# Attention: score rows of the second block folded to their 128 visible columns by a predicated copy, and the transposed blocks parted by GpSimd

## The reference

```python
qi = jnp.arange(WINDOW)[:, None]              # WINDOW = 128
kj = jnp.arange(2 * WINDOW)[None, :]
rel = qi + WINDOW - kj
sc = jnp.einsum('bqkgd,bjkd->bkgqj', qx, kx) * scale
valid = (rel >= 0) & (rel < WINDOW) & (blk * WINDOW + kj - WINDOW >= 0)
sc = jnp.where(valid[None, None, None], sc, NEG_INF)
p = jax.nn.softmax(jnp.concatenate([sc, sink_logits], axis=-1), axis=-1)[..., :-1]
return jnp.einsum('bkgqj,bjkd->bqkgd', p.astype(vx.dtype), vx)
```

## Time and profile before

| | us |
|---|---|
| median of three runs | 1015.26 (1015.19 to 1015.81) |
| the profiled execution | 1015.4 |
| its span, first to last instruction | 1013.6 |
| TensorE busy | 1009.5 |
| VectorE busy | 786.3 |
| ScalarE busy | 497.2 |
| GpSimd busy | 101.4 |

### The profile page before, as it was taken

One profiled execution on the slowest core, in us unless ns is written; L12 is line 12 of the kernel. 1 busy time (PEld: TensorE's weight loads), 2 busy tenths in 40 slices (PEclk: granted clock), 3 DMA queues, 4 the chain that ended last, 5 costly groups with the idle time before them and its releaser, 6 DMA issues.

```text
span 1013.6 us, 15818 instructions
## 1 busy us (share of the span) xinstructions
PE 1009.5 (100%) x5916; PEld 886.5 (87%) x5916; DVE 786.3 (78%) x886; ACT 497.2 (49%) x537; POOL 101.4 (10%) x103
## 2 busy tenths in 40 slices
PE   9999999999999999999999999999999999999998
PEld 8888888888888888888888888888897898888888
DVE  7988866797797878777767787787778977977743
ACT  7455435544443354454444454464447944544432
POOL 0000013201101052000013100001220041000000
PEclk9999999999999999999999999999999999999999
DMA  9664456652542454555455645535562344644461
GB/s 348 242 237 177 143 174 218 246 197 104 218 195 97 193 171 173 212 190 180 150 179 199 246 166 201 191 135 172 187 244 115 110 160 188 208 168 166 156 193 64
DMA packets 32295, 185.31 MB, mean 183 GB/s; under 512 B 3840, under 2 KB 6400, under 8 KB 16128
## 3 DMA queue, kind: packets, MB, share of 16 engines
q1 hardware_dynamic: 31968, 184.64, 50.9%
q10 hardware_dynamic: 288, 0.16, 0.1%
HBM read 183.73 MB, written 1.05 MB: 182 GB/s over the span
## 4 chain that ended last, share of the span: by engine, by line
PE 100%; DVE 0%; issue 0%; DVEq 0%
PE ps L1219 99%; PE ps L1585 1%; PE ps L1552 0%; PE ps L1544 0%; DVE x L841 0%; DVE ones L1125 0%; DVEq L1126 0%
## 5 line engine op out<-in xcount | busy, mean ns | idle before, releaser
L1219 PE MATMUL ps<-h,w_hi 128*128 128x512 f32 x1664 | 556.1, 393 | 0.0
L1219 PE MATMUL ps<-h,w_lo 128*128 128x256 f32 x1664 | 430.8, 279 | 0.0
L658 DVE TENSOR_TENSOR w_lo<-stage,w_hi 128x2048 fp32r<-128x2048 f32 (+1 forms) x190 | 398.2, 2105 | 29.3 <-ACT w_hi L339 29.1
L1219 PEld LDWEIGHTS ps<-h,w_hi 128*128 128x128 f32 x1664 | 310.1, 188 | 66.9 <-DVE w_lo L658 0.2
L339 ACT ACTIVATE w_hi<-stage 128x2048 fp32r<-128x2048 f32 (+1 forms) x190 | 326.7, 1727 | 5.6 <-PE ps L1219 4.7
L1219 PEld LDWEIGHTS ps<-h,w_lo 128*128 128x128 f32 x1664 | 302.1, 189 | 3.5
L1219 PE MATMUL ps<-act_t,w_hi 128*128 128x512 f32 (+1 forms) x726 | 240.0, 386 | 0.0
L1219 PE MATMUL ps<-act_t,w_lo 128*128 128x256 f32 x704 | 190.1, 279 | 0.0
L1219 PEld LDWEIGHTS ps<-act_t,w_hi 128*128 128x128 f32 x726 | 134.4, 188 | 28.4
L371 ACT ACTIVATE tmp<-ps 128x1024 f32<-128x1024 f32 x44 | 45.1, 1026 | 189.2 <-PE ps L1219 189.2
L1219 PEld LDWEIGHTS ps<-act_t,w_lo 128*128 128x128 f32 x704 | 130.4, 189 | 0.3
(11 more groups left out here) (172 smaller groups left out, 746.9 us busy)
## 6 DMA issues: line engine op xcount, KB each, us to landing
stage<-w_in_dram SPq DMA_DIRECT2D x85, 1024.0 KB, 4.8
stage<-w_out_dram SPq DMA_DIRECT2D x64, 704.0 KB, 4.0
stage<-w_ret_dram SPq DMA_DIRECT2D x24, 1024.0 KB, 4.9
stage<-w_ret_out_dram SPq DMA_DIRECT2D x8, 1024.0 KB, 4.8
stage<-w_q_dram SPq DMA_DIRECT2D x4, 1024.0 KB, 6.3
stage<-w_o_dram SPq DMA_DIRECT2D x4, 1024.0 KB, 4.9
stage<-w_in_dram SPq DMA_DIRECT2D x8, 256.0 KB, 4.2
stage<-w_in_dram SPq DMA_DIRECT2D x2, 512.0 KB, 6.1
```

Source lines behind the costliest of these rows:

```text
L658: nc.vector.tensor_tensor(w_lo[:, s, 0:n], stage[:, s, 0:n], w_hi[:, s, 0:n].bitcast(F32), ALU.subtract).then_inc(lo_ready, 1)
L1219: return nc.tensor.matmul(out_, w, x_, start=start, stop=stop)
```

## The change

In the second block a query sees exactly one of the two keys at each position modulo 128. Now the scores of both blocks are computed without a mask product, and VectorE copies, where the old mask of the own block is not zero, the score of the earlier block over that of the own block: a predicated copy in PSUM. Maximum, exponential, scaling and transposes then work on 128 columns a head instead of 256. The transposed block is copied by ScalarE to the second half of `pt_two`; GpSimd multiplies it with a 0/1 triangle to get the part that belongs to the earlier block, and subtracts that from the whole to get the other part. The value products stay as they were, but wait for GpSimd (`p_second`) and not for ScalarE. The first half of the mask constant becomes the 0/1 triangle.

```diff
-    s_two = [at(f"s_two{c}", [P, CH, 2 * P], F32, (big + 20480, base + 110592)[c]) for c in range(2)]
+    s_two = [at(f"s_two{c}", [P, CH, P], F32, (big + 20480, base + 110592)[c]) for c in range(2)]
...
+    def row_scores(e, j):
+
+        return scores(e, j)[:, keys(e) - P:keys(e)]
...
-                    nc.scalar.activation(s[:, j, :], scores(e, j), ACT.Exp, bias=sm[:, e, 1, j:j + 1],
+                    nc.scalar.activation(s[:, j, :], row_scores(e, j), ACT.Exp, bias=sm[:, e, 1, j:j + 1],
...
-                first = h0 + heads * r
+                first = h0 + 4 * r
...
-                nc.scalar.activation(pt[:, first:first + heads, :, :],
-                                     ps[:, P_T_BANKS[e][r], :].rearrange("p (a k n) -> p a k n", a=heads, n=P),
+                nc.scalar.activation((pt_two if b else pt_own)[:, first:first + 4, b, :],
+                                     ps[:, P_T_BANKS[e][r], :].rearrange("p (a n) -> p a n", n=P),
                                      ACT.Copy).then_inc(pt_ready[e][r], 1)
...
...
-                chain.step(nc.vector.tensor_reduce(mx.rearrange("q (i p) -> q i p", p=2), scores_by_head(e), AX.X,
-                                                   ALU.max))
+                by_head = scores_by_head(e)
+                if b:
+                    chain.step(nc.vector.copy_predicated(
+                        by_head[:, :, :, P:2 * P],
+                        mask[:, P:2 * P].bitcast(I32).rearrange("q (i p k) -> q i p k", i=1, p=1).broadcast_to(
+                            [P, n // 2, 2, P]), by_head[:, :, :, 0:P]))
+                    by_head = by_head[:, :, :, P:2 * P]
+                chain.step(nc.vector.tensor_reduce(mx.rearrange("q (i p) -> q i p", p=2), by_head, AX.X, ALU.max))
...
+            def blocks_of_p(n, e):
+
+                c, b, h0, heads = SOFTMAXES[e]
+                first, second = (pt_two[:, h0:h0 + heads, kb, :] for kb in range(2))
+                pool.wait_ge(pt_ready[e][0], 1)
+                nc.gpsimd.tensor_tensor(first, second, same(mask[:, 0:P], heads), ALU.mult).then_inc(p_first, 1)
+                pool.wait_ge(p_first, n + 1)
+                nc.gpsimd.tensor_tensor(second, second, first, ALU.subtract).then_inc(p_second, 1)
+
+            pool.wait_ge(mask_loaded, 48)
             pool.wait_ge(rope_loaded, 32)
...
             square_sum(ATT)
+            for n, e in enumerate((TWO_0A, TWO_0B, TWO_1A, TWO_1B)):
+                blocks_of_p(n, e)
             square_sum(5)
...
-                                  False, j >= h0 + n - 2)
+                                  bool(b), bool(b) or j >= h0 + n - 2)
...
-                    pe.wait_ge(pt_ready[e][0], 1)
-                    pe.wait_ge(pt_ready[e][1], 1)
+                    pe.wait_ge(p_second, 2 * c + k % 2 + 1)
...
-                masks(TWO_0A)
-                masks(TWO_0B)
-                transposed_p(TWO_0A, 1)
-                transposed_p(TWO_0B, 1)
-                pe.wait_ge(pt_ready[TWO_0B][0], 1)
-                pe.wait_ge(pt_ready[TWO_0B][1], 1)
-                masks(TWO_1A)
-                pe.wait_ge(pt_ready[TWO_0A][1], 1)
                 transposed_p(OWN_0, 1)
+                pe.wait_ge(pt_ready[TWO_0B][0], 1)
                 head_scores(TWO_1A)
-                masks(TWO_1B)
-                transposed_p(TWO_1A, 1)
-                pe.wait_ge(pt_ready[TWO_1A][1], 1)
-                transposed_p(TWO_1B, 1)
...
+    mask[:, 0:P] = np.arange(P)[:, None] > np.arange(P)[None, :]
```

More of the change, by code:

```diff
@@ L234, in trunk @@
     p_scaled, p_ready = sem("p_scaled"), sem("p_ready")
+    p_first, p_second = sem("p_first"), sem("p_second")
     pt_done, pt_ready = ([[sem(f"{n}{e}{r}") for r in range(2)] for e in range(len(SOFTMAXES))]
@@ L548, in rows_of_p @@
                 c, b, h0, n = SOFTMAXES[e]
-                pt = pt_two if b else pt_own
-                heads = 4 // (1 + b)
-                first = h0 + heads * r
+                first = h0 + 4 * r
                 if c:
@@ L582, in attention @@
                 rows_of_p(TWO_0A, 0)
-                rows_of_p(TWO_0A, 1)
                 rows_of_p(TWO_0B, 0)
-                rows_of_p(TWO_0B, 1)
                 squares(1, 1)
@@ L599, in attention @@
                 rows_of_p(TWO_1A, 0)
-                rows_of_p(TWO_1A, 1)
                 rows_of_p(OWN_1, 1)
@@ L604, in attention @@
                 rows_of_p(TWO_1B, 0)
-                rows_of_p(TWO_1B, 1)
                 split(v + 1)
@@ L1055, in softmax_back @@
                 nc.vector.tensor_tensor(
-                    s, s, sm[:, e, 4, h0:h0 + n].rearrange("p (g a) -> p g a", a=1).broadcast_to([P, n, keys(e)]),
+                    s, s, sm[:, e, 4, h0:h0 + n].rearrange("p (g a) -> p g a", a=1).broadcast_to([P, n, P]),
                     ALU.mult).then_inc(p_ready, 1)
@@ L1558, in masks @@
                 c, b, h0, n = SOFTMAXES[e]
-                own = mask_r[:] if b else mask_r[:, P:2 * P]
                 for bank in SCORE_BANKS[e]:
-                    matmul(ps[:, bank, 0:n // 2 * keys(e)].rearrange("p (a n) -> p a n", a=n // 2), ident_r[:],
-                           same(own, n // 2), True, False)
+                    matmul(ps[:, bank, :].rearrange("p (a n) -> p a n", a=n // 2), ident_r[:],
+                           same(mask_r[:, P:2 * P], n // 2), True, False)
             def head_scores(e):
@@ L1582, in transposed_p @@
                 for q in range(4):
-                    tile = 4 * r + q
-                    head, kb = (tile // 2, tile % 2) if b else (tile, 0)
                     last = nc.tensor.transpose(ps[:, P_T_BANKS[e][r], q * P:(q + 1) * P],
-                                               s[:, h0 + head, kb * P:(kb + 1) * P], ident[:])
+                                               s[:, h0 + 4 * r + q, :], ident[:])
                 last.then_inc(pt_done[e][r], 1)
```

## The result

The changed kernel took 1024.80 us (median of 6 runs, 1023.88 to 1029.43) against 1015.22 (1014.93 to 1015.81) for the kernel before in the same comparison: ratio 1.0098, interval [1.0087, 1.0109]. It is slower; 1023.5 had been forecast. Five of the six runs lie between 1023.88 and 1024.98; the profiled one is the sixth, 1029.43, with a span of 1027.6 us, so its trace holds some 5 us that the typical run does not.

What follows compares the result with a forecast made beforehand. TensorE was taken as busy nearly throughout, with VectorE also at its limit in the attention stage. Holds and waits from GpSimd, less saved transposes, summed to +8.2 us on the profiled 1015.4: 1023.5 us predicted, range 1019 to 1026.

Steps and rivals of the forecast that it cites:

- What bounds the stage: Attention stage: up to the first output tile TensorE can't run ahead of VectorE, so work removed there turns into waiting.
- rival C: Attention stage: the whole removed TensorE work pays, 1011.8 us; chance 0.04.
- B: Rival at the value products: GpSimd's pair of operations is hidden, not slower, -0.5 us, 1014.9; chance 0.07.
- A: Rival: no exclusion between GpSimd and VectorE, only GpSimd's latency counts, +0.8 us, 1016.2; chance 0.12.
- D: Rival: only TWO_1A and TWO_1B cost, where splits collide with GpSimd; +5.3 us, 1020.7; chance 0.77 together with the forecast.
- place 1: TWO_0A and TWO_0B: GpSimd holds VectorE's rope addition and OWN_0 multiplication, +3.1 us, delaying the first output tile.
- VectorE's part of the fold: Four fronts: predicated copy 0.68 us added, maximum halved from 1.22 to 0.69, +0.2 us a front.
- Place 2: TWO_1A: two GpSimd operations and VectorE's split share the port; TensorE's value products wait 3.0 us.
- Place 3: TWO_1B: GpSimd's operations and VectorE's splits hold each other; TensorE's value products wait 2.8 us.
- the sum: Attention stage: +3.1 + 0.2 - 0.44 + 3.0 - 0.44 + 2.8 = +8.2 us on the profiled 1015.4.

Runs made afterwards that it cites:

- e6: Kernel before with the eight mask products of the second block's softmaxes left out, scores unmasked: 1015.73 us, ratio 1.0002.
- e1: Changed kernel without GpSimd's eight operations; value products take the whole transposed block for both key blocks: 1015.42 us, ratio 0.9999.
- e2: Changed kernel with GpSimd's eight operations going into a tile nobody reads, value products not waiting for them: 1019.84 us, ratio 1.0041.
- e0: Changed kernel run again, unedited: 1023.83 us, ratio 1.0093 against the kernel before.
- e3: Changed kernel with 35 unneeded mask products filling TensorE's four waits: 1024.13 us, ratio 1.0085.
- e9: Changed kernel with another VectorE order behind TWO_1B, the last two output divisions each ahead of a split: 1020.62 us, ratio 1.0052.
- e5: Changed kernel with VectorE multiplying from PSUM, GpSimd making only the difference of the value blocks, used as weight: 1017.86 us, ratio 1.0021.
- e4: Changed kernel with GpSimd only multiplying, the subtraction moved into the value products: 1019.18 us, ratio 1.0040.

## Why the prediction was right

The forecast was 1023.5 us; the median was 1024.8, and 1023.83 when run again. By its own steps:

**What bounds the stage.** VectorE does up to the first output tile. e6 shows it by itself: 1.8 us less on TensorE, no change. e1 shows that the whole removed work, with VectorE's copies beside it, is worth nothing, so rival C is out. B is out by the waits of 2.89 and 2.54 us for GpSimd, A by e2, and D by place 1, which costs 3.1 us with nobody waiting for GpSimd there.

**VectorE's part of the fold.** Copy and maximum each 0.69 us (0.68 and 0.69 taken). The first tile of e1 is 0.3 us late, where the walk had 0.2 to 0.3.

**Place 1.** +3.1 forecast, 3.1 in e0 and 3.2 in e3. In the profiled run 0.28 of it is there when the rope addition starts, and the hold adds 0.97 at the rope addition, 1.06 at the small sum and 0.79 at the multiplication. The order came as written (rope addition, GpSimd's second, TWO_0B's first, multiplication for OWN_0). One detail was wrong: the small sum does not slip in; it has two SBUF inputs and took 1.22 us, until GpSimd's second had ended. It cost nothing more, since the multiplication behind it would have been held in its place.

**Place 2.** A wait of 3.0 forecast, 2.89 in e0 and in the profiled run. The hold of 1.14 us charged for an operation behind a split was 1.12. Undisturbed operations took 1.26 to 1.27 us, 1.83 times VectorE's 0.69, so the 1.14 charged for every operation was 0.12 short where no split stood ahead of it. By the Trainium skill's "GPSIMD Engine Reference", section "4.1 Engine selection", about twice VectorE's time for two inputs, the estimate had been 1.4 us, above those rows.

**Place 3.** 2.8 forecast, 2.54 in the profiled run, with the order of the walk to the instruction (first operation, split, second operation). The typical run e0 has no such wait, but half clock in its stead. e3, which has the waits and no fall of the clock, is the clean test of the sum: 1024.13 - 1015.37 = 8.8 us against 8.2.

**What the sum left out.** The clock. The forecast said that no row told what waits of 3 us do to it and put no price on it. It goes with the spread from 1023.5 to 1029.4: in the two traces the fall comes behind one wait (e0) or behind two (the run of 1029.43), and there it costs 2.15 and 2.9 us, or next to nothing where half-speed work covers a wait that would have come anyway (e0). The clock averaged over a run goes with the time: 0.997 in the runs of 1023.48 to 1023.88, 0.995 in those of 1024.72 to 1027.48, 0.993 in the one of 1029.43. So the sum was right, as e3 shows, but that the typical run lands on it as well is partly luck: in e0 the half clock costs about what the third wait would have cost, and the forecast had put no price on it. Why the clock falls behind the wait of 2.23 us in one run and not in the other is not settled here.

## What to carry to other kernels

Before shortening TensorE's stream, ask in that stage whether TensorE could run ahead: e6 took 1.8 us of products away and got nothing. An idle GpSimd is not free capacity: an operation that read SBUF there held each VectorE instruction with two SBUF inputs that it met for about as long as it had left to run (0.8 to 1.1 us here, for a sum of 128x8 too), and half the loss (e2, with the half clock behind it) came with nobody waiting for its result. If it must run, place it where VectorE reads PSUM or has one SBUF input; another order of VectorE's splits (e9) took more than 3 us off.

## What the runs showed of the hardware beyond that

TensorE's granted clock fell from 1.00 to 0.50 behind waits of 2.2 to 2.9 us, and stayed there for 6 us in the profiled run of the changed kernel and in e0, with TensorE busy for 5.8 to 6.0 of them; in e5 and e9 for about 3. In e9 it fell only when TensorE had been back at work for about a microsecond (transposes at 793.06, granted clock 1.00 from 793 to 794 and 0.53 from 794 to 795). The wait of 2.23 us has another of 1.27 us ahead of it, with 0.66 us of transposes between them, in the profiled run as in e0. In e4 it fell where waits of 1.27 and 1.45 us followed one another:

```profile
790.51 0.66 PE L1570 MATMUL ps<-ident,q_a 128*128 128x128 f32 x4 [1.27 <-ACT q_sq L523]
792.62 1.94 PE L1600 MATMUL ps<-ident,s_own 128*128 128x128 f32 x8 [1.45 <-DVE s_own L1061]
```

Products that nobody needs, put into the waits (e3), kept it at 1.000 and narrowed the runs from 1023.5 to 1029.4 down to 1023.9 to 1024.6, at no gain in the median. Whether they would pay where the waits are longer was not tried.
